# Expert rows scattered with addition into x in memory, experts p and p+16 as a pair, and other engines clearing the semaphores

## What is computed

```python
g_sel = jnp.argmax(g_logits, axis=-1)
p_g = jnp.max(jax.nn.softmax(g_logits, axis=-1), axis=-1)
e_in = e_logits[jnp.arange(n_tok), g_sel]          # 8 experts of the group
top_v, top_i = lax.top_k(e_in, 2)
top_w = jax.nn.softmax(top_v, axis=-1) * p_g[:, None]
expert_id = g_sel[:, None] * 8 + top_i
gates = sum over both picks of one_hot(expert_id, 32) * top_w
act = jax.nn.silu(x @ w_gate[e]) * (x @ w_up[e]) * gates[:, e]
y = sum over experts e of act @ w_down[e]           # 1024 -> 256 -> 1024
```

## Time and profile before

| | us |
|---|---|
| median of three runs (1483.66 to 1489.05) | 1488.04 |
| the profiled execution | 1488.0 |
| its span | 1486.4 |
| PE busy | 1222.6 (82%) |
| DVE, ACT, POOL busy | 371.5, 246.5, 230.6 |
| mean granted clock of TensorE | 0.911 |

### The profile page before, as it was taken

The page is one execution under the profiler, slowest core; times in us unless marked ns, Lnnn a source line. Parts: engine busy times, 40 slices in busy tenths (PEclk is TensorE's granted clock), DMA queues, the critical chain, the costliest instruction groups (busy, mean ns, idle before and its releaser), DMA issues. The chain is left out here.

```text
span 1486.4 us, 15915 instructions
## 1 busy us (share of the span) xinstructions
PE 1222.6 (82%) x6119; PEld 648.3 (44%) x6119; DVE 371.5 (25%) x808; ACT 246.5 (17%) x571; POOL 230.6 (16%) x288
## 2 busy tenths in 40 slices
PE   6999998887879499788845999998869679887860
PEld 4765674555634433223213764445734433322220
DVE  4132004544301611111105400112610521111115
ACT  2000005642302101000003201014410301000001
POOL 2300003312100011111012000203810011111003
PEclk9999999999989789989975999998979889999895
DMA  8320665659874569999938131302156659999946
GB/s 271 97 65 23 240 275 185 193 181 364 291 289 199 215 259 421 421 421 420 419 106 296 40 112 23 127 0 79 44 212 259 233 200 416 420 420 421 420 164 205
DMA packets 105421, 350.99 MB, mean 236 GB/s; under 512 B 21406, under 2 KB 40034, under 8 KB 80634
## 3 DMA queue, kind: packets, MB, share of 16 engines
q1 hardware_dynamic: 87576, 304.43, 53.2%
q0 software_dynamic: 17472, 45.37, 8.6%
q10 hardware_dynamic: 290, 0.07, 0.0%
HBM read 320.09 MB, written 44.41 MB: 245 GB/s over the span
## 5 line engine op out<-in xcount | busy, mean ns | idle before, releaser
L1197 PE MATMUL ps<-moe_gu,rows 128*64 128x512 f32 x1024 | 256.0, 658 | 64.5 <-DMA moe_gu<-in_moe_w_up 59.4
L1197 PEld LDWEIGHTS ps<-moe_gu,rows 128*64 128x64 f32 x1024 | 78.8, 151 | 219.3 <-issue 155.3
L1132 PE MATMUL ps<-moe_gu,turned 128*128 128x512 f32 x256 | 115.5, 615 | 12.6 <-DMA moe_gu<-in_fox_w_out 7.0
L1700 PE MATMUL ps<-mwblk,turned 128*128 128x512 f32 x256 | 111.5, 593 | 2.2 <-DVE vaug L1862 1.5
L1093 POOL DMA_INDIRECT expert_rows<-turned,moe_dst_row x32 | 32.0, 999 | 397.7 <-ACT turned L1301 390.1
L1468 DVE TENSOR_TENSOR turned<-turned,ps 128x256 f32<-128x256 f32 x32 | 13.5, 422 | 319.9 <-ACT turned L1291 319.9
L1132 PEld LDWEIGHTS ps<-moe_gu,turned 128*128 128x128 f32 x256 | 50.4, 198 | 76.7 <-issue 63.5
L1213 PE MATMUL ps<-moe_wd,moe_rowsel 128*64 128x512 f32 x352 | 80.4, 598 | 2.4 <-ACT turned L1301 2.4
L1700 PEld LDWEIGHTS ps<-mwblk,turned 128*128 128x128 f32 x256 | 48.0, 190 | 61.0 <-issue 57.4
L1291 ACT ACTIVATE turned<-ps 128x256 f32<-128x256 f32 x32 | 12.3, 383 | 329.2 <-PE ps L1197 329.2
L355 PE MATMUL ps<-turned,fox_arena 128*128 128x288 f32 x256 | 63.1, 407 | 0.0
(11 more groups left out here) (343 smaller groups left out, 1460.0 us busy)
## 6 DMA issues: line engine op xcount, KB each, us to landing
moe_gu<-in_moe_w_gate SPq DMA_DIRECT2D x64, 1024.0 KB, 22.2
moe_gu<-in_moe_w_up SPq DMA_DIRECT2D x64, 1024.0 KB, 24.3
moe_wd<-in_moe_w_down SPq DMA_DIRECT2D x44, 1024.0 KB, 25.6
rows<-in_moe_w_down SPq DMA_DIRECT2D x20, 1024.0 KB, 25.1
fox_arena<-in_cache_k SPq DMA_DIRECT2D x32, 512.0 KB, 8.9
fox_arena<-in_cache_v POOLq DMA_DIRECT2D x32, 512.0 KB, 9.4
fox_arena<-in_fox_w_in SPq DMA_DIRECT2D x6, 2048.0 KB, 10.2
expert_rows<-x SPq DMA_DIRECT2D x6, 2048.0 KB, 22.7
```

The costliest lines, as they stand in the source:

```text
L1132: mm = pe.matmul(ps[:, 2 * n + half, :], turned[:, c, n * P:(n + 1) * P], w[:, c, half * 512:half * 512 + 512], start=(c == 0), stop=(c == ...
L1197: mm = pe.matmul(ps[h, 2 + p % 2, :].rearrange("s (k f) -> s k f", k=2), xT[:, c, h], gu[s][:, half, :, c, :], start=(c == 0), stop=(c == ...
L1700: mm = pe.matmul(ps[:, m % 4, :], turned[:, c, n * P:(n + 1) * P], wblk[:, k % 3, c, :], start=(c == 0), stop=(c == KC - 1))
```

## The change

x is no longer combined from gathered rows. The x tiles are written to memory (`x_rows`, with 128 rows behind the last token for empty slots); the share of each slot's token is computed by PE into `slot_gate` and multiplied into the hidden values; and each tile's 128 result rows are scattered to their tokens' rows of `x_rows` by an indirect DMA that adds (`compute_op=ALU.add`). Every scatter waits until the one before has landed. Empty slots add to the extra rows instead of being skipped. A pair is now experts p and p+16, which lie in different groups, so that no token occurs twice in a scatter. When all have landed, SP loads the five x tiles back. `fill_rows` and its 13.1 MB are gone; 1 MB is written to the extra rows instead.

Beside this: a fourth down buffer (the space of x); gate and up of pairs 3 and 15 are loaded in halves, the first half of pair 3 already when half of `gate_up` of pair 0 is done; `tilesel` is made in two wide instructions and the shares are computed before its result is read; the mLSTM phase computes half of the gates after the third tile and half of the first keys after the fourth; its weight blocks wait for nothing; and the semaphores are cleared by ACT (expert phases, mLSTM projections, `finish`) or SP (mLSTM cells), up to 62 of them.

```diff
-SET = 50
+SET = 62
...
-        def fill_rows(sp):
...
+        def fill_trash(sp):
+
+            for to in x_dram:
+                sp.dma_start(to[TOK:TOK + P, :], x[:, 0, :]).then_inc(filled, 16)
...
+            wd.append(x[:, 0:4, :].rearrange("p (h m) d -> p h m d", h=2))
+            DOWNS = len(wd)
...
+            def keep_x_tile(sp, n):
+
+                sp.wait_ge(added, n + 1 if n < L else L + 2)
+                sp.dma_start(x_dram[layer][n * P:n * P + ROWS[n], :], x[0:ROWS[n], n, :]).then_inc(x_kept, 16)
...
+                for n in range(NT):
+                    keep_x_tile(sp, n)
                 sp.wait_ge(flipped, NT)
                 sp.wait_ge(kept, 16 * NT)
                 load_down(sp, 2)
-                for p in range(SLOTS, STATIC + 1):
-                    if p < STATIC:
+                sp.wait_ge(x_kept, 16 * NT)
+                load_down(sp, 3)
+                for p in range(SLOTS, STATIC):
+                    if p in FINE:
+                        for u in range(2):
+                            sp.wait_ge(gu_half if p == SLOTS and u == 0 else gu_done, p - SLOTS + 1)
+                            load_gate_up_part(sp, p, u)
+                    else:
                         sp.wait_ge(gu_done, p - SLOTS + 1)
                         load_gate_up(sp, p)
-                    if p > SLOTS:
-                        sp.wait_ge(y_done, p - SLOTS)
-                        load_down(sp, p - 1)
+                    if p >= DOWNS:
+                        sp.wait_ge(y_done, p - DOWNS + 1)
+                        load_down(sp, p)
...
+                sp.wait_ge(scattered, 1)
+                for n in range(NT):
+                    sp.dma_start(x[0:ROWS[n], n, :], x_dram[layer][n * P:n * P + ROWS[n], :]).then_inc(x_back[layer][n], 16)
...
-                pool.indirect_dma_start(y_dram, bass.IndirectOffsetOnAxis(ap=dst_row[:, p:p + 1], axis=0), y[:, s, :], None,
-                                        bounds_check=TILES * SLOT - 1, oob_is_err=False).then_inc(landed, 16)
+                pool.indirect_dma_start(x_dram[layer], bass.IndirectOffsetOnAxis(ap=rows_of, axis=0), y[:, s, :], None,
+                                        bounds_check=TOK + P - 1, oob_is_err=True, compute_op=ALU.add).then_inc(landed, 16)
+
+            def scatter_static(pool, p):
+
+                if p == 0:
+                    pool.wait_ge(x_kept, 16 * NT)
+                else:
+                    pool.wait_ge(y_out[(p - 1) % 2], 16 * ((p - 1) // 2 + 1))
+                scatter(pool, p, p % 2, dst_row[:, p:p + 1], y_out[p % 2])
...
+                pe.wait_ge(gates_ready, 1)
+                for k in range(2 * NT):
+                    for h in range(2):
+                        mm = pe.matmul(ps[h * SLOT:(h + 1) * SLOT, 7, 0:TILES // 2], rowsel[:, k, :], hit[:, k, h:TILES:2],
+                                       start=(k == 0), stop=(k == 2 * NT - 1))
+                mm.then_inc(gates_done, 1)
...
+                    if p == 0 and c == KC // 2 - 1:
+                        mm.then_inc(gu_half, 1)
...
-                    dve.tensor_scalar(tilesel[:, k, :], const("iota_tile"), s10["tl"][:, j, n:n + 1], const("token")[:, n:n + 1],
-                                      ALU.is_equal, ALU.mult).then_inc(sel_ready, 1)
...
+                ch(dve.tensor_tensor(hit, const("iota_tile").unsqueeze(1).broadcast_to([P, 2 * NT, TILES]),
+                                     tl.broadcast_to([P, 2 * NT, TILES]), ALU.is_equal))
...
+                dve.scalar_tensor_tensor(hid[:], sg[:], slot_gate[:, p:p + 1], ps[:, 2 + p % 2, HID:2 * HID], ALU.mult, ALU.mult
+                                         ).then_inc(a_ready, 1)
...
-                    gather_back(pool, yg[k][0:ROWS[n], :], n, j, yg_in[k])
...
+                    if n == 2:
+                        pe.wait_ge(wg_in, 80)
+                        pe.wait_ge(gained, 3)
+                        gates_half(pe, 0)
+                    if n == 3:
+                        pe.wait_ge(w_in[0], 16)
+                        first_half(pe, 0)
...
-                    act.wait_ge(combined, 2 * n + 2)
+                    act.wait_ge(x_back[0][n], 16)
...
-                if who == "pool" and n:
+                if who == phase.get("clears", "pool") and n:
                     for s in sets[(n - 1) % 2][0:len(taken[n - 1])]:
                         eng.sem_clear(s)
```

More of the change, by code:

```diff
@@ L85, in constants @@
     c["iota_slot"][:] = np.arange(SLOT)
-    c["iota_tile"][:] = np.arange(TILES)
+    tile = np.arange(TILES)
+    c["iota_tile"][:] = np.where(tile < EXP, tile // 2 + (tile % 2) * STATIC, tile)
     c["rev4"][:] = GROUPS - np.arange(GROUPS)
@@ L91, in constants @@
     c["token"][:] = np.where(tok < TOK, tok - NOWHERE, 0)
-    c["own_row"][:] = np.arange(TILES // 2)[None, :] * P + i
+    c["trash"][:] = TOK + i
+    c["other"][:] = np.where(i // SLOT == np.arange(2)[None, :], 0, NOWHERE)
     c["minus_half"][:] = -0.5
@@ L161, in trunk @@
         half = sb("half", [P, 1])
-        slot = sb("slot", [P, 2, NT], U32)
-        share = [sb(f"share{j}", [P, NT]) for j in range(2)]
+        share = sb("share", [P, 2, NT])
         def const(name, p=P):
@@ L179, in trunk @@
         filled = lasting("filled")
-        def fill_rows(sp):
[L183 to L188, removed]
+        def fill_trash(sp):
+            for to in x_dram:
+                sp.dma_start(to[TOK:TOK + P, :], x[:, 0, :]).then_inc(filled, 16)
+        x_back = [[lasting(f"x_back{layer}_{n}") for n in range(NT)] for layer in range(2)]
         def log_sigmoid_act(act, neg_abs, e, u, lnu, bent, rounded, logged):
@@ L1617, in pool_ @@
             def pool_(pool):
-                for k in range(2 * NT):
-                    n, j = divmod(k, 2)
-                    gather_back(pool, yg[k][0:ROWS[n], :], n, j, yg_in[k])
                 for n in range(NT):
@@ L1713, in wide, with gates_half, first_half @@
                 mm.then_inc(done, 1)
+            def gates_half(pe, half):
+                for c in range(KC):
+                    mm = pe.matmul(ps[0:64, 6 + half, 0:HT], wg[:, c, :], turned[:, c, half * HT:(half + 1) * HT],
+                                   start=(c == 0), stop=(c == KC - 1))
+                if half:
+                    mm.then_inc(g_done, 1)
+            def first_half(pe, half):
+                for c in range(KC):
+                    mm = pe.matmul(ps[:, 4 + half, 0:HT], wblk[:, 0, c, 0:P], turned[:, c, half * HT:(half + 1) * HT],
+                                   start=(c == 0), stop=(c == KC - 1))
+                if half:
+                    mm.then_inc(k_done, 1)
             def pe_(pe):
@@ L1880, in dve_ @@
                 ch.wait()
-            phases.append(dict(sp=sp_, pool=pool_, pe=pe_, act=act_, dve=dve_))
+            phases.append(dict(sp=sp_, pool=pool_, pe=pe_, act=act_, dve=dve_, clears="act"))
         def mlstm():
@@ L2328, in dve_ @@
                 stage(dve, MPAIRS - 1)
-            phases.append(dict(sp=sp_, pool=pool_, pe=pe_, act=act_, dve=dve_))
+            phases.append(dict(sp=sp_, pool=pool_, pe=pe_, act=act_, dve=dve_, clears="sp"))
             ms_.close()
@@ L2337, in finish @@
             L = NT - 1
-            yg = sb("f_yg", [P, 2 * NT, D], where=fin)
             gl = sb("gl", [P, D], where=fin)
-            combined, yg_in = sem("f_combined"), [lasting(f"f_yg_in{k}") for k in range(2 * NT)]
             gl_in, squared, meaned, rooted, ended, y_out = (sem("gl_in"), sem("f_squared"), sem("f_meaned"), sem("f_rooted"),
@@ L2377, in dve_ @@
             def dve_(dve):
-                for n in range(NT):
-                    for j in range(2):
-                        k = 2 * n + j
-                        combine(dve, yg[0:ROWS[n], k, :], n, j, yg_in[k], 0, combined)
-                        if j == 0 and n:
-                            mean(dve, n - 1)
-                    if n == 0:
-                        dve.wait_ge(gl_in, 16)
-                    else:
-                        end(dve, n - 1)
-                mean(dve, L)
+                dve.wait_ge(gl_in, 16)
+                mean(dve, 0)
+                for n in range(1, NT):
+                    mean(dve, n)
+                    end(dve, n - 1)
                 end(dve, L)
-            phases.append(dict(sp=sp_, pool=pool_, act=act_, dve=dve_))
+            phases.append(dict(sp=sp_, pool=pool_, act=act_, dve=dve_, clears="act"))
             fin.close()
```

176 lines of the change are left out of this document (89 added, 87 removed).

## The result

| | before | after |
|---|---|---|
| median | 1485.09 us (20 runs, 1479.81 to 1489.05) | 1491.54 us (20 runs, 1486.8 to 1494.62) |
| the profiled execution, its span | 1488.0, 1486.4 | 1490.26, 1488.6 |

The ratio is 1.0038, with an interval of 1.0027 to 1.0049. The change makes the kernel 0.4% slower; the forecast was 1475.5, 0.8% faster. The time lies just above the range. Gains and losses nearly cancel; six stretches of the profiled executions show where each one is. The profiled executions differ by 2.2 us and the medians by 6.5, so 4 us of the difference stand in no row. "Last copy" is the end of the copy that the last scatter waits for; "keys" is the first use of the mLSTM phase's keys by ACT.

The account below looks back on a forecast made before the run. DMA was taken to bound most of each expert phase, serial chains the two stretches behind them. Two phases at +11 us, minus 14 and 20.5 at the ends, gave -12.5 us: 1475.5 us, range 1440 to 1490.

Parts of the forecast that it names:

- The sum: Whole kernel: two expert phases at +11 us each, minus 14 between the layers and 20.5 at the end, -12.5 us.
- Part 1: The end, last scatter to span end: without gathers and their DVE chain, gain 20.5 us, bounds 14 and 24.
- Part 2: Between the layers, barrier to first mLSTM keys: squares start sooner and PE works in halves, gain 14 us, bounds 9 and 17.
- the routing's +2.2: Routing ahead of the expert phases: two wide instructions before PE can begin, +1.1 us a layer.
- Part 5: What costs nothing: dropping `fill_rows`, SP's clears in the mLSTM cells, each scatter's wait for the one before (landing 10.5 us).
- The prediction's signs of being wrong: Starved pairs' period stays at 17 us or passes 19, or the squares wait for x.
- Part 4: Added in expert phases: routing +1.1 us a layer; adding rows at two packets, period 18.6, +19 us a layer.
- (a): Rival, scatters in the full DMA stretch: an adding row costs one packet, 1444 us; chance 0.27 including prices up to two.
- (b): Rival, scatters in the full DMA stretch: an adding row costs three packets or more, 1507 us at three; chance 0.13.
- (c): Rival, expert phases: the chain of scatters bounds if one lands after more than 17 us, 1534 at 20; chance 0.03.
- (d): Rival, both ends: they give 23 us instead of 34.5, x landing late or ACT clearing slowly, 1487; chance 0.05.
- Part 3: Full DMA stretch of the expert phases: fourth down buffer 5 us, early half some 4 us, saved 9 us a layer.

Follow-up runs that it names:

- The best kernel: Kernel after, with empty slots skipped, alternating pairs (wait for the scatter two before), PE clearing at both ends, final gain row loaded before the x loads: 1471.92 us, ratio 0.9896.

## Why the prediction was wrong

**The sum** had -12.5 us; the profiled execution shows +2.2 and the medians +6.5. Parts 1 and 2 fell short by 6.6 and 7.2 us, the two expert phases cost 4.8 us more than their +19.8, and two stretches that no part named came out 3.9 us shorter than the routing's +2.2 (-1.7 instead), which is within what they vary by.

**Parts 1 and 2** failed at the stations before the first square; behind it the forecast held in the mLSTM phase and was 1.3 us short in finish. Part 1 let the wait for the last scatter end "about 1.5 us later" and POOL's drain follow at once: barrier 8.8 us behind the last copy. It was passed 15.1 us behind it (1471.50 - 1456.41), in three pieces:
- *The last scatter waits for its neighbour*: issued 3.0 us behind the copy, not 0.8. Part 5 costed this wait at nothing, as one scatter lands in 10.5 us and a pair takes 12 to 17. That holds inside the phase. But nothing stands between the last two scatters except a `down`: their issues would be 4.8 us apart, and the first needs 6 even with idle engines. 2.2 us here, 2.4 in the mLSTM phase; the alternating order took it away, 2.6 us at each end.
- *Issue and landing*: 6.04 us from the start of the issue, against 3.6 before: 2.5 us more where 1.5 were taken. 0.6 of it is POOL's issue, 1.56 us instead of 0.97.
- *The barrier stands behind SP's five loads*: 6.0 us from the landing to the barrier, where 2.8 were forecast. Part 1 spoke of SP issuing the loads "meanwhile", beside POOL's drain. But the barrier waits for SP too, and SP comes to it only behind its 2.3 us of issues and its own drain. 3.2 us here, 3.5 in the mLSTM phase. Moving the loads behind the barrier didn't help, since then the squares wait for x.

ACT's clears took the forecast's 4 us (3.9), and x was in time. Behind the first square, finish took 9.8 us instead of 8.5, and what follows the last product took 0.9 less than before, so that 6.3 + 1.3 - 0.9 make the 6.6 within 0.1. `gl` has 0.6 us of the 1.3: it had been covered before by ten gathers, and the change took the cover away. No part named it. In the kernel after ACT's clears still hid most of it; once they were moved to PE, loading it early was worth 3.6 us of finish. The rest goes to POOL's roots, 1.52 us beside DVE's final products, where the forecast had 0.9 for a mean and a root together.

Part 2 failed with the same three pieces, 2.4, 1.3 (the last scatter landed after 6.4 us) and 3.5 us, about 7 in all; from the first square to the keys it was 33.7 us against the forecast's 32 to 33.

The best kernel's end takes 25.8 us from the last copy, a gain of 20.3 against the 20.5 of Part 1. That is luck. Its barrier is passed 12.8 us behind the last copy and not 8.8, as the late landing and SP's five loads are still there, and what pays for them are the 4 us of clears that Part 1 had on the path and that PE now does aside.

The prediction's signs of being wrong did not come: the period neither stayed at 17 nor passed 19, and the squares did not wait for x. Barrier to first keys took 37.4 us where 37 were forecast. The loss lay ahead of the barrier, and of all the signs only the time from the last scatter to the end of the span, 29.2 us instead of 25, took it in.

**Part 4** was right, and it was the term with most at stake. An adding row takes 0.33 us, the engine time of two plain rows. Taking the addition away gave 14 us a layer; the forecast's step from one to two packets is 19 - 4 = 15 us. The period of 18.3 to 18.5 and the landing of 10.5 us were near the forecast's. The Trainium skill, "Collectives: The Full Stack" (The bandwidth ceiling), says that a collective's adding step delivers about half of what its copy does, since it reads two sources with two descriptors a chunk. The rate in this case's trace agrees, 0.33 us a row against 0.164; two descriptors do not show in it, as the packet count is the same with and without the addition. What the prediction called a second packet is there as time and not as a packet. Rivals (a), (b) and (c) are out. The case was nearest to (d), the ends give less, held at 0.05: it gave 1487 with both ends at their lower bounds (23 us); they gave 20.7, and by neither of its reasons, as x was not late and ACT's clears were not slow.

**Part 3** has its early half confirmed at 3.5 to 4.7 us a layer. But without the addition a layer's phase is only 1.2 and 2.5 us shorter than before, where one packet a row was to bring 5 (9 saved, 4 added). So 3 us a layer of the 9 did not come; which of the buffer, the x tiles in the routing or the scatters took them is not settled, the run with three buffers having changed the order of waits too.

**Part 5**: nothing shows a cost of the fill or of the clears by SP, though 1 us could not be seen in the stretches that hold them. It was wrong of the wait between scatters, at its last link alone.

## What to carry to other kernels

When a combination moves from gathers into adding scatters, the full DMA stretch pays for it: each row costs twice, and here this ate the 20 us that the ends gave. Two parts that stood beside it (clears on an idle engine, an early half) gave 1473.7 us alone, which cannot be told from the best version with the scatters, 1471.9. At a phase's end, walk through the last two items, not the steady state: a chain of waits that is free inside the loop shows there, a barrier stands behind everything that any of its engines still issues, and a small load behind the barrier becomes the bound as soon as the work that covered it is gone.

## What the runs showed of the hardware that was not expected

- An adding row of 4 KB is one packet of 0.33 us (a plain one 0.164), and POOL's issue of an adding scatter takes 1.56 to 1.59 us against 0.97 to 1.02 of a plain one. At the ends, with no weights left to load, it lands 5.9 to 6.5 us after the start of its issue, a plain one of as many rows after 3.3.
- Skipping empty slots freed 1.05 us of each engine a pair and shortened a starved pair by 0.3 us in layer 1 and by nothing in layer 0.
- PE takes about 7.1 us for 58 semaphore clears, ACT 3.9, POOL 3.0 for its 46.
- POOL's root of one column takes 0.57 us while DVE is idle and 1.52 us beside DVE's final products (chain of the kernel after: 1477.40 and 1479.42). It took 0.54 in the kernel before, though an addition of DVE had begun 0.04 us earlier (1469.88 and 1469.92); what decides is not shown.
